# Attention scores on half the rows and value products on half the columns of TensorE, in a two-layer streaming encoder step

## What is computed

```python
A_HEADS, A_KV_HEADS, A_HEAD_DIM, CHUNK, WIN_ROWS = 16, 4, 64, 64, 128
s = einsum('bnikgd,bnjkd->bnkgij', qb, kb) * (A_HEAD_DIM ** -0.5)   # 4 query heads share one key/value head
s = s - slopes[:, :, None, None] * dist                             # ALiBi
s = where(key_ok, s, -1e30)                                         # own chunk and the two before
p = softmax(concatenate([s, sink], axis=-1), axis=-1)[..., :-1]
o = einsum('bnkgij,bnjkd->bnikgd', p, vb)
```

## Time and profile before

| | before |
|---|---|
| median of 3 runs | 1680.62 us (1679.03 to 1684.2) |
| span of the profiled execution | 1679.0 us, 1.6 us less than the median |
| attention (first score matmul to the next stage's first matmul) | 139.3 to 497.6 us |
| busy, of the span | PE 93%, weight loads 88%, DVE 57%, POOL 41%, ACT 27% |
| mean granted TensorE clock | 0.966 of full |
| HBM | 53 GB/s over the span |

### The profile page before, as it was taken

The page is one execution under the profiler, slowest core; times in us unless marked ns, Lnnn a source line. Parts: engine busy times, 40 slices in busy tenths (PEclk is TensorE's granted clock), DMA queues, the critical chain, the costliest instruction groups (busy, mean ns, idle before and its releaser), DMA issues.

```text
span 1679.0 us, 24582 instructions
## 1 busy us (share of the span) xinstructions
PE 1554.7 (93%) x9460; PEld 1477.9 (88%) x9460; DVE 951.6 (57%) x1456; ACT 449.8 (27%) x798; POOL 684.5 (41%) x461
## 2 busy tenths in 40 slices
PE   6998989899998997979999999988999999989995
PEld 6997878788777997978998999988999999989994
DVE  6215757576775365553726610168887878884114
ACT  5112323233343212122124100123425143361000
POOL 5252212221112232431423644445666566657551
PEclk9999999999998998999999999999999999999997
DMA  4211010101000000100110322211111111113222
GB/s 172 84 57 38 14 41 25 41 13 40 26 15 31 32 30 31 37 30 31 41 33 26 131 88 80 89 40 42 59 51 51 38 51 51 51 55 100 89 77 107
DMA packets 27416, 89.71 MB, mean 53 GB/s; under 512 B 3600, under 2 KB 6736, under 8 KB 27344
## 3 DMA queue, kind: packets, MB, share of 16 engines
q1 hardware_dynamic: 16560, 60.34, 10.6%
q10 hardware_dynamic: 10784, 28.39, 5.1%
HBM read 77.16 MB, written 11.68 MB: 53 GB/s over the span
## 4 chain that ended last, share of the span: by engine, by line
PE 54%; DVE 11%; issue 5%; ACT 3%; POOL 2%; ACTq 0%; POOLq 0%; DVEq 0%
PE ps L345 40%; PE ps L392 5%; DVE arena L1193 2%; PE ps L510 1%; POOL w_hi L316 1%; DVE Y L1444 1%; PE ps L570 1%; PE ps L575 1%; POOL w_lo L320 1%; PE ps L559 1%; DVE arena L1462 1%; PE ps L470 1%; PE ps L443 1%; DVE arena L1506 1%; DVE H L1025 1%
## 5 line engine op out<-in xcount | busy, mean ns | idle before, releaser
L316 POOL TENSOR_TENSOR w_hi<-raw,ones 128x512 fp32r<-128x512 f32 x228 | 335.6, 1472 | 941.5 <-PE ps L345 535.9
L345 PE MATMUL ps<-H,w_hi 128*128 128x364 f32 x2832 | 578.3, 331 | 32.1 <-DVE H L1025 20.9
L345 PEld LDWEIGHTS ps<-H,w_hi 128*128 128x128 f32 x2832 | 485.8, 189 | 38.3 <-issue 22.4
L345 PE MATMUL ps<-H,w_lo 128*128 128x364 f32 x1752 | 388.4, 330 | 0.0
L320 POOL TENSOR_TENSOR w_lo<-raw,w_hi 128x512 fp32r<-128x512 f32 x228 | 350.2, 1536 | 17.9
L345 PEld LDWEIGHTS ps<-H,w_lo 128*128 128x128 f32 x1752 | 307.1, 190 | 0.0
L345 PE MATMUL ps<-Yr,w_hi 128*128 128x364 f32 x672 | 149.1, 330 | 0.0
L510 PE MATMUL ps<-H,w_hi 128*128 128x364 f32 x672 | 148.0, 347 | 0.0
L392 PE MATMUL ps<-w_hi,H 128*128 128x256 f32 (+1 forms) x720 | 132.1, 284 | 7.3 <-POOL w_lo L320 6.6
L1366 DVE TENSOR_TENSOR arena<-ps,arena 128x1092 f32 (+1 forms) x16 | 20.7, 1295 | 206.7 <-PE ps L345 206.7
L790 ACT ACTIVATE arena<-arena,sm 128x256 f32<-128x256 f32 (+1 forms) x144 | 69.6, 484 | 241.6 <-DVE sm L1140 241.6
(11 more groups left out here) (180 smaller groups left out, 1932.4 us busy)
## 6 DMA issues: line engine op xcount, KB each, us to landing
raw<-weights SPq DMA_DIRECT2D x114, 512.0 KB, 3.3
arena<-xT ACTq DMA_DIRECT2D x15, 546.0 KB, 4.8
x_scratch<-arena ACTq DMA_DIRECT2D x8, 546.0 KB, 5.4
arena<-x_scratch ACTq DMA_DIRECT2D x8, 546.0 KB, 3.6
yT<-arena ACTq DMA_DIRECT2D x8, 546.0 KB, 2.9
arena<-k_scratch ACTq DMA_DIRECT2D x8, 304.0 KB, 4.6
k_scratch<-Y ACTq DMA_DIRECT2D x2, 512.0 KB, 2.7
arena<-xT SPq DMA_DIRECT2D x1, 546.0 KB, 4.9
```

The costliest lines, as they stand in the source:

```text
L316: pool.tensor_tensor(w_hi[:, s, cols].rearrange("p (k n) -> p k n", n=P), raw[:, s, cols].rearrange("p (k n) -> p k n", n=P), every_tile_ones,
L345: mm = pe.matmul(sets[st][:, c, 0:CW], lw[:, s, w], rx[:, k, c * CW:(c + 1) * CW], start=(first and n == 0 and m == 0), stop=(last and n = ...
```

## The change

The keys are kept as `kk`, one copy on partitions 0 to 63 and one on 64 to 127, and the values as `Vg`, 64 columns per tile, both without zeros. `scores` issues two matmuls, one per head j: q and kk on partitions 64j to 64j+63, output of head j in bank 3 + j. So one unit uses both banks, and it now waits for VectorE's reading of the unit before (`s_free` at U + 2). For the ninth tile the left operand is 68 columns wide, of which VectorE reads 64. `mix_values` issues the same number of matmuls, each with 64 columns of values, head j into partitions 64j to 64j+63 of bank 7, with a `start` and `stop` for each head. The memsets and `a_zeroed` go; ScalarE's first key load waits for `h_lo_done` and `sq_done`, since `kk` lies where the input X was.

```diff
--- before.py
+++ after.py
@@ -194,8 +194,8 @@
 
         KW = SEQ + WIN + DEC
         q = part(0, 2, TOK)
-        kz = part(2184, 2, KW)
-        Vz = part(4616, 10, 192)
+        kk = part(2184, KW)
+        Vg = part(4616, 10, 64)
         Ssb = part(6536, 3, 2, 256)
         PT = part(8072, 2, 512)
 
@@ -431,17 +431,19 @@
                 in_block(1 - n % 2, n % 2, PC_A + n, USE_A[n % 2] + n // 2)
             pe.wait_ge(v_free, NT)
             pe.wait_ge(drained[1], USE_A1[1])
-            pe.wait_ge(a_zeroed, 3)
 
             def scores(u, U):
                 t, b = unit(u)
-                r = tile_rows(t)
-                pe.wait_ge(s_free, U + 1)
+                r = TOK - SEQ if t == NT - 1 else P
+                pe.wait_ge(s_free, U + 2)
                 k0, k1, c0 = (SEQ, KW, 0) if t == NT - 1 else ((t - 1) * P, (t + 1) * P, 0)
                 if t == 0:
                     k0, c0 = 0, P
-                pe.matmul(ps[0:r, 3 + u % 2, :].rearrange("p (j n) -> p j n", j=2)[:, :, c0:c0 + k1 - k0],
-                          q[:, b, t * P:t * P + r], kz[:, :, k0:k1], start=True, stop=True).then_inc(s_done, 1)
+                for j in range(2):
+                    h = slice(A_DIM * j, A_DIM * (j + 1))
+                    mm = pe.matmul(ps[0:r, 3 + j, c0:c0 + k1 - k0], q[h, b, t * P:t * P + r], kk[h, k0:k1],
+                                   start=True, stop=True)
+                mm.then_inc(s_done, 1)
 
             def key_tiles(t):
 
@@ -467,9 +469,9 @@
                 tiles = key_tiles(t)
                 for n, (kt, tile, rows) in enumerate(tiles):
                     for j in range(2):
-                        mm = pe.matmul(ps[:, 7, 0:r], Vz[0:rows, tile, 64 * (1 - j):64 * (1 - j) + P],
+                        mm = pe.matmul(ps[A_DIM * j:A_DIM * (j + 1), 7, 0:r], Vg[0:rows, tile, :],
                                        PT[0:rows, u % 2, (2 * kt + j) * P:(2 * kt + j) * P + r],
-                                       start=(n == 0 and j == 0), stop=(n == len(tiles) - 1 and j == 1))
+                                       start=(n == 0), stop=(n == len(tiles) - 1))
                 mm.then_inc(o_done, 1)
 
             def low_rank(h, before):
@@ -733,10 +735,11 @@
 
             def load_keys(g):
                 for j in range(2):
-                    act.dma_start(kz[64 * j:64 * j + 64, j, :], one(k_all, g)).then_inc(kz_in, 16)
+                    act.dma_start(kk[A_DIM * j:A_DIM * (j + 1), :], one(k_all, g)).then_inc(kk_in, 16)
 
             act.wait_ge(k_all_in, 80)
-            act.wait_ge(a_zeroed, 3)
+            act.wait_ge(h_lo_done, KD)
+            act.wait_ge(sq_done, KD)
             load_keys(0)
             act.wait_ge(rt_done, 1)
             for t in range(NT):
@@ -1056,12 +1059,8 @@
 
 
             dve.wait_ge(h_lo_done, KD)
-            dve.memset(kz[64:P, 0, :], 0.0).then_inc(a_zeroed, 1)
-            dve.memset(kz[0:64, 1, :], 0.0).then_inc(a_zeroed, 1)
-            dve.memset(Vz[:, :, :], 0.0).then_inc(a_zeroed, 1)
             dve.tensor_scalar(nsink[:, :], vecs[:, VC_SINK:VC_SINK + A_HEADS], -1.0, None, ALU.mult)\
                .then_inc(sink_neg, 1)
-            dve.wait_ge(a_zeroed, 3)
             dve.wait_ge(sink_neg, 1)
 
             dve.wait_ge(rb_done, 1)
@@ -1090,8 +1089,8 @@
             def attend(g, more):
                 U = ATT_UNITS * g
                 dve.wait_ge(gated, 2 * g + 2)
-                dve.tensor_copy(Vz[:, 0:9, 64:128], V[:, 0:9, bass.ds(A_DIM * g, A_DIM)])
-                dve.tensor_copy(Vz[0:64, 9, 64:128], V[0:64, 9, bass.ds(A_DIM * g, A_DIM)]).then_inc(vz_ready, 1)
+                dve.tensor_copy(Vg[:, 0:9, :], V[:, 0:9, bass.ds(A_DIM * g, A_DIM)])
+                dve.tensor_copy(Vg[0:64, 9, :], V[0:64, 9, bass.ds(A_DIM * g, A_DIM)]).then_inc(vg_ready, 1)
                 dve.tensor_copy(cur_sink[:, 0, :], vecs[:, bass.ds(VC_SINK + 4 * g, 4)])
                 dve.tensor_copy(cur_sink[:, 2, :], consts[:, bass.ds(CC_SLOPE + 4 * g, 4)])
                 dve.tensor_copy(cur_sink[:, 1, :], nsink[:, bass.ds(4 * g, 4)]).then_inc(sink_cur, 1)
@@ -1127,7 +1126,7 @@
                         for j in range(2):
                             last = dve.scalar_tensor_tensor(
                                 Ssb[0:r, r3, j, c0:c1], dist[0:r, c0:c1], cur_sink[0:r, 2, 2 * b + j:2 * b + j + 1],
-                                ps[0:r, 3 + s % 2, j * 256 + c0:j * 256 + c1], ALU.mult, ALU.add)
+                                ps[0:r, 3 + j, c0:c1], ALU.mult, ALU.add)
                         last.then_inc(s_free, 1)
                         dve.wait_ge(s_free, U + s + 3)
 
```

More of the change, by code:

```diff
@@ L250, in build_program @@
         vecs_in, consts_in, wlr_in, vcache_in = sem("vecs_in"), sem("consts_in"), sem("wlr_in"), sem("vcache_in")
-        k_all_in, kz_in, gstate_in = sem("k_all_in"), sem("kz_in"), sem("gstate_in")
+        k_all_in, kk_in, gstate_in = sem("k_all_in"), sem("kk_in"), sem("gstate_in")
         res_in = [sem("res_in0"), sem("res_in1")]
@@ L265, in build_program @@
         v_done, v_free = sem("v_done"), sem("v_free")
-        a_zeroed, vz_ready, gate_tanh = sem("a_zeroed"), sem("vz_ready"), sem("gate_tanh")
+        vg_ready, gate_tanh = sem("vg_ready"), sem("gate_tanh")
         gated, blr_ready, es_done = sem("gated"), sem("blr_ready"), sem("es_done")
@@ L487, in attend @@
                 pe.wait_ge(drained[0], USE_A1[0] + 4 * g)
-                pe.wait_ge(kz_in, 32 * g + 32)
-                pe.wait_ge(vz_ready, g + 1)
+                pe.wait_ge(kk_in, 32 * g + 32)
+                pe.wait_ge(vg_ready, g + 1)
                 U = ATT_UNITS * g
@@ L830, in decays @@
                 act.activation(E, E, ACT.Exp, scale=1.0 / GATE_NORM).then_inc(e_done, 1)
-            act.wait_ge(vz_ready, A_KV)
+            act.wait_ge(vg_ready, A_KV)
             act.wait_ge(o_free, A_KV * ATT_UNITS + 1)
@@ L1175, in _ @@
             dve.wait_ge(k_saved, 32)
-            dve.wait_ge(vz_ready, A_KV)
+            dve.wait_ge(vg_ready, A_KV)
             dve.memset(Y[:, KD:MIX, LIVE:TOK], 0.0).then_inc(y_zeroed, 1)
```

## The result

The change makes the kernel faster: 1657.78 us median (1652.72 to 1658.58, 4 runs) against 1679.82 (1678.37 to 1684.2, 4 runs), a ratio of 0.9869 with a 95% interval of 0.9852 to 0.9886. I had forecast 1688, with 1666 to 1710 as range: wrong in sign, and outside the range. The span of the profiled execution fell from 1679.0 to 1655.8 us.

The account below looks back on a forecast made before the run. PE's work per step was taken to bound the attention. Full tiles +7.8, first +3.9, ninth -3.1 gave +8.6 us, +7.5 on the path; 1679.0 + 7.5 = 1686.5, on the median's scale 1688 us, range 1666 to 1710.

Parts of the forecast that it names:

- What bounds the kernel: Attention: PE's own work per step sets its length, except in a few steps where PE waits for VectorE.
- The change of shape: PE leaving the full array and coming back costs 0.33 us, paid twice by every unit; bounds 0.25 and 0.35.
- The failed step: Full units on PE: score passes take three slots, 0.645 us for 0.86; value passes five slots, 0.515 us for 0.82.
- four cases: Overlap of the heads: forecast's own slots 0.53, both wholly at once 0.20, none 0.15, only one piece overlapping 0.12.
- The rival without any overlap: Scores and values: the halves take turns, +36.5 us on the path, 1717 us; chance 0.15.
- Removed zeroing: Three memsets on VectorE go; they were already covered by its wait for ScalarE's factors: 0 us.
- fast rival: Scores and values: both heads run wholly at once, -19 us against the forecast's own case, 1669 us; chance 0.20.
- the group starts stay as they are: Four group starts: unchanged, since PE waits there for VectorE's copy of the values, not the reverse.
- One score buffer less: Score matmuls wait for VectorE's reading of the unit before, not of the one before that: costs nothing.
- The ordinary step: PE's step in the attention: 4.61 us before, forecast to become 4.75 us.
- First and ninth tiles: Scores and values: first tiles +0.49 us each, +3.9 over 8 units; ninth tiles -0.39 each, -3.1 over 8.

Follow-up runs that it names:

- e5: Changed kernel with both matmuls of a pair on the same half, head 1's own scores and output left out: 1705.5 us, ratio to before 1.0159.
- e1: Changed kernel with the three memsets put back on VectorE at their old place, on memory that nothing reads: 1665.09 us, ratio to before 0.9918.
- e2: Kernel before with the zeroing of kz and Vz done by ScalarE instead of VectorE's memsets: 1672.26 us, ratio 0.9962.
- e8: Kernel before with the score matmul waiting for VectorE's reading of the unit before, not of the one before that: 1678.8 us, ratio 0.9998.
- e6: Changed kernel with PE's value products right behind the scores and the transposes last, three shape changes a step instead of four: 1659.47 us, ratio 0.988.
- e9: e6 with ScalarE's copy of the transposed probabilities moved ahead of the exponentials: 1647.63 us, ratio to before 0.9824.
- e3: Kernel before with only the scores on half the rows, values zero-padded as before, one memset left on VectorE: 1675.76 us, ratio 0.9979.
- e4: Kernel before with only the value products on half the columns, keys zero-padded as before, two memsets left on VectorE: 1672.82 us, ratio 0.9974.
- e7: The changed kernel itself, run again as the base for other runs: 1657.07 us, ratio to before 0.9867.
- e10: Changed kernel with ScalarE's copy moved ahead of the exponentials, PE's order as in the change: 1654.02 us, ratio 0.987.

## Why the prediction was wrong

- **What bounds the kernel**: right. PE's own work per step set the attention's length; what its step lost, the kernel gained, besides the stall.
- **The change of shape**: right in kind and size. 0.33 us for a way in and out was forecast from one case in the earlier trace rows and two in the earlier trace rows; it is 0.31 on the mean, paid twice a step, 0.36 for the row halves and 0.25 for the column halves. The Trainium skill, "TensorEngine Tiling (Array Packing)", Key Properties, says that changing the tiling mode drains the engine; the trace agrees, with 0.17 to 0.33 us without a weight load ahead of each of the four pieces.
- **The failed step**: "I take b's first pass as going beside a's second: three slots of 0.215", and five slots for the values. It rested on the order a, a, b, b, for which I had no row. The trace shows two slots and four. Per full unit that is 0.215 and 0.103 us, which turns +0.14 into -0.18; measured is -0.19. e5 shows the same from the other side: with both matmuls of a pair on one half each piece takes 0.43 us more. I had this case as a rival, with 0.20 and -11.4 us for it (7.5 - 19, before rounding 18.9); in e1, which has the halves without the other effect, the attention is 11.2 us shorter and the median 13.8 lower. Its price was about right and its chance was not: no row of before bore on the question, so four cases should have stood nearer to even. The rival without any overlap is what e5 runs: 28 us above the kernel before, where I had 36.5; the stall (7 us) and the cheaper change of shape are the difference.
- Whether the passes leave as a, b, a, b or each half is served without regard to the other's order stays open: starts 0.007 us apart tell only that they overlap. The Trainium skill, "TensorE: Matmul & The Clock Gate", What overlaps and what doesn't, has matmuls start and end in program order; that does not speak against the trace if the two passes of an fp32 matmul are not bound together, which no run here shows. The Trainium skill, "TensorEngine Tiling (Array Packing)", Key Properties, says that tiles work independently; e5 agrees, with 0.43 us per piece.
- **Removed zeroing: 0**: wrong, and it is why the time lies outside even the fast rival's 1669. The memsets' own 3.8 us were covered, as I wrote. What I left out is that removing instructions moves the rest of that engine's program. The stalls stood in the trace of before (3.54 and 3.52 us with no releaser ahead of L1093, 1.7 to 2.0 ahead of L1096), and I had written that the group starts stay as they are. e1 and e2 put this at 7.3 and 6.6 us, of which 5.9 and 5.4 are PE's longer idle at the two returns. With 7 us off, the fast rival's 1669 becomes 1662; most of what is left to 1657.8 is that the halves gave 13.8 us by e1's median, not 11.4.
- **One score buffer less: 0**: right (e8, ratio 0.9998; PE's wait for L1127 in the changed kernel is 0.5 us in all).
- **The ordinary step** was given as 4.61 us; start to start it is 4.69 with 15 projection matmuls, and one step in five has 12. The error came from multiplying 0.167 instead of reading two starts, and did no harm to a sum of differences. The value passes of before are 0.11 us apart, not 0.103; the projection's first record starts only 0.03 us behind the last of them.
- **First and ninth tiles**: forecast +0.49 and -0.39 a unit. Measured, a first tile's scores went from 0.43 to 0.42 and its values stayed at 0.37, with 0.25 us of entering and leaving around them; a ninth's scores went from 0.79 to 0.48 and its values from 1.07 or 1.17 to 0.53.

## What to carry to other kernels

Two small matmuls on different halves of the array pay only where they run at once, and only if the pair's saved streaming exceeds what the shape costs on the way in and out: here 0.43 against 0.36 us for the scores and 0.38 against 0.25 for the values. Put the pieces of other shapes next to each other so that there are fewer changes, and then look at what waits in the new order, as e6 and e9 show. When a change shortens an engine's program, compare the idle times without a releaser at loop returns before the gain is put down to the change.

## What was not expected of the hardware

- A pair of fp32 matmuls on two halves overlaps in both its passes (starts 0.007 us apart), so that 4 passes of 0.215 us take two slots. On the same half they take four (1.06 instead of 0.63 us).
- Row halves to column halves is one change of shape (e6: 4.31 us a step against 4.50), not two by way of the full array.
- The way in and out costs 0.36 us for row halves (e3) and 0.25 for column halves (e4). The first weight load, 0.107 us until the next for 128 columns and 0.055 for 64, is not hidden there.
- VectorE's stall of 3.4 to 4.1 us at a loop's return comes and goes with what stands ahead of the loop: present in before, e1, e3, e4 and e8, with 23 to 25 packets on the second instruction queue; absent in the changed kernel, e2, e5, e6, e7, e9 and e10, with 13 or 14. In each of the ten stalls two packets of that queue start while VectorE stands still, and at the fourteen returns without a stall there is none. A second, shorter idle lies ahead of the loop's fourth instruction in four of these kernels and ahead of the fifth in e3 (1.49 us before L1099), which has two memsets fewer than before. So the stall goes with transfers of a queue that the profile calls one for instructions. That VectorE waits for just these, and that the length of its program decides it and not where the loop comes to lie, is argued, not shown.
- The idle's length alone does not tell the clock behind it. After 5.0 to 5.5 us of PE's idle (ten returns in before, e1, e3, e4, e8) the granted clock was 0.50 from the first pass on. After 2.1 to 2.4 us (fourteen returns in the other seven) PE started at full speed in five places, and in the rest at half speed within 0.2 us, with both in executions of the same kernel (after and e7).
